# Early split weights and first taps on ScalarE, the first token tile routed ahead, and router scores issued in small steps between expert rows

## What is computed

```python
hn = rms_norm(h, norm_mix_g);  proj = hn @ w_in
xv, bg, cg, ga, gg = split(proj)
y_sc = bg * causal_conv3(cg * xv)                               # 3 taps
y_cf = silu(layer_norm(causal_conv31(ga * sigmoid(gg)) + b))    # 31 taps
h = h + concat(rms_norm(y_sc), rms_norm(y_cf)) @ w_out
hn = rms_norm(h, norm_ffn_g)
q  = hn @ peer_w_q                       # 8 heads of 256
s1, s2 = q[:, :128] @ K1.T, q[:, 128:] @ K2.T     # 128 scores each, per head
idx, gates = top16 of (top16(s1) + top16(s2)), softmax
h = h + sum over 8 heads x 16 of  gelu(u[idx] . hn) * gates * v[idx]
x = final_norm(h)
# second block: ffn1, two attention mixers with gates, ffn2, in fp32
```

## Time and profile before

| | |
|---|---|
| median of 3 runs | 2622.81 us (2619.71 to 2624.23) |
| profiled execution, its own time | 2621.03 us |
| span of that execution, first to last instruction | 2619.2 us |
| granted TensorE clock, mean | 0.913 |
| busy: PE, DVE, ACT, POOL | 83%, 69%, 45%, 29% of the span |
| DMA moved | 758.77 MB, mean 290 GB/s |

### The profile page before, as it was taken

The page is one execution under the profiler, slowest core; times in us unless marked ns, Lnnn a source line. Parts: engine busy times, 40 slices in busy tenths (PEclk is TensorE's granted clock), DMA queues, the critical chain, the costliest instruction groups (busy, mean ns, idle before and its releaser), DMA issues.

```text
span 2619.2 us, 28482 instructions
## 1 busy us (share of the span) xinstructions
PE 2164.6 (83%) x9496; PEld 1516.6 (58%) x9496; DVE 1808.6 (69%) x3312; ACT 1172.9 (45%) x3766; POOL 765.1 (29%) x634
## 2 busy tenths in 40 slices
PE   6986988877777776999674588799919998899999
PEld 6965433332222223885332477588419977698997
DVE  5995366568988886786798987667574545556554
ACT  4223344556666665332354653333244435344443
POOL 0000253444555555333444643333320001100000
PEclk9988999999999998999785579899969998899999
DMA  4220698899999999999997999999974542115453
GB/s 169 81 81 32 235 374 353 319 363 421 421 421 421 408 420 375 389 421 387 374 371 271 367 374 421 378 419 421 392 310 144 181 176 107 65 65 193 145 179 143
DMA packets 107170, 758.77 MB, mean 290 GB/s; under 512 B 12032, under 2 KB 12800, under 8 KB 16400
## 3 DMA queue, kind: packets, MB, share of 16 engines
q0 software_dynamic: 73728, 536.90, 50.7%
q1 hardware_dynamic: 33296, 220.05, 22.3%
HBM read 754.81 MB, written 2.10 MB: 289 GB/s over the span
## 4 chain that ended last, share of the span: by engine, by line
PE 40%; DVE 11%; DMA 4%; issue 3%; ACT 1%; POOL 1%; DVEq 0%; ACTq 0%
PE bank L541 39%; DVE resid L942 4%; DMA pair<-in_uv,idx 4%; DVE pair L1504 2%; DVE half L936 1%; DVE tmp L936 1%; PE bank L902 0%; PE bank L561 0%; DVE smalls L1220 0%; ACT frow L1577 0%; ACT half L1577 0%; DVE smalls L1293 0%; DVE ft_lo L936 0%; POOL smalls L2014 0%; DMA raw<-in_wts 0%
## 5 line engine op out<-in xcount | busy, mean ns | idle before, releaser
L2058 POOL DMA_INDIRECT pair<-in_uv,idx x512 | 654.8, 1279 | 933.9 <-DVE resid L942 588.7
L1577 ACT ACTIVATE smalls<-smalls 128x1 f32<-128x1 f32 x2058 | 540.1, 286 | 660.1 <-DVE smalls L1504 642.2
L1504 DVE CUSTOM_DVE_ANT_0 pair<-pair,hn 128x1024 f32<-128x1024 f32 x512 | 624.3, 1220 | 177.2 <-DMA pair<-in_uv,idx 175.6
L541 PE MATMUL bank<-pair,diag 128*128 128x512 f32 x960 | 480.2, 637 | 158.7 <-ACT diag L1577 158.4
L541 PEld LDWEIGHTS bank<-pair,diag 128*128 128x128 f32 x960 | 175.3, 197 | 459.8 <-ACT diag L1577 320.0
L942 DVE SCALAR_TENSOR_TENSOR resid<-pair,smalls,resid 128x1024 f32<-128x1024 f32 x272 | 348.1, 1280 | 46.4 <-ACT smalls L1577 46.2
L541 PE MATMUL bank<-ft,raw 128*128 128x256 f32 x1664 | 366.1, 384 | 11.9 <-DVE ft L936 11.9
L541 PEld LDWEIGHTS bank<-ft,raw 128*128 128x128 f32 x1664 | 320.5, 193 | 57.3 <-issue 12.7
L936 DVE TENSOR_TENSOR half<-raw,half 128x1024 fp32r<-128x1024 f32 (+1 forms) x212 | 244.5, 1195 | 135.6 <-ACT half L1577 135.6
L541 PE MATMUL bank<-ft_hi,half 128*128 128x256 f32 x1664 | 299.4, 282 | 6.4 <-DVE ft_lo L936 6.4
L1577 ACT ACTIVATE half<-raw 128x1024 fp32r<-128x1024 f32 (+1 forms) x212 | 207.7, 1030 | 164.8 <-PE bank L541 156.8
(11 more groups left out here) (252 smaller groups left out, 2587.4 us busy)
## 6 DMA issues: line engine op xcount, KB each, us to landing
raw<-in_wts SPq DMA_DIRECT2D x194, 1024.0 KB
pair<-in_uv,idx POOLq DMA_INDIRECT x512
raw<-in_wts SPq DMA_DIRECT2D x10, 512.0 KB
raw<-in_wts SPq DMA_DIRECT2D x4, 720.0 KB
resid<-in_x SPq DMA_DIRECT2D x4, 512.0 KB, 5.7
out<-resid SPq DMA_DIRECT2D x8, 256.0 KB, 6.2
raw<-in_wts SPq DMA_DIRECT2D x2, 768.0 KB
rowt<-in_rows SPq DMA_DIRECT2D x1, 1076.0 KB, 12.6
```

The costliest lines, as they stand in the source:

```text
L541: return e.matmul(o, a, b, start=start, stop=stop)
L1504: e.tensor_tensor_reduce(b[:, 0:1024], b[:, 0:1024], HN[i // 128], 1.0, 0.0, ALU.mult, ALU.add, actv[:, i % 8:i % 8 + 1]).then_inc(dotted, 1)
L1577: return e.activation(o, i, f, **kw)
L2058: e.indirect_dma_start(pair[i % NPAIR], None, uv, bass.IndirectOffsetOnAxis(ap=idx[:, n % SLOTS, k:k + 1], axis=0)).then_inc(pairs_in[i % ...
```

## The change

- `half` has four buffers while chunks 0 to 7 are split. Chunks 1, 2 and 3 are split ahead of the first gated product, and chunk 13 ahead of the variance.
- The first tap of each of the eight convolution pieces is done by ScalarE (`tap`).
- The `y_cf` products, the sum into `resid` and the norm of tile 0 stand first; tiles 2 and 3 follow the route of head 0.
- `CALLS`: heads 0 and 1 for tile 0 alone before row 0; heads 2 to 7 for all tiles; then heads 0 and 1 for tiles 1 to 3, for which two weight chunks (`wr`, the same data as `wq` 0 and 1) are loaded a second time.
- `scores_in_steps(n + 2)` runs in step n, for n from 0 to 7: on PE 2 of its matmuls follow each of rows 0 to 7, and the key products rows 10 and 11; ScalarE's four copies follow rows 5, 9, 13 and 14.
- One route a step until step 7 (it was 5), two in steps 8 to 15, none in 16 and 17, one in 18 to 24 (it was 18 to 22). In steps 0 to 7 a route starts at row 2 of its step.
- Every fourth row is added by VectorE until row 127 (it was 95).

```diff
-ON_PE = [i < HALF + 8 and not (i < 96 and i % 4 == 3) for i in range(PAIRS)]
+ON_PE = [i < HALF + 8 and not (i < 128 and i % 4 == 3) for i in range(PAIRS)]
-    ROUTES.append(list(range(_at, min(32, _at + (1 if _n < 6 else 2 if _n < 16 else 0 if _n < 18 else 1)))))
+    ROUTES.append(list(range(_at, min(32, _at + (1 if _n < 8 else 2 if _n < 16 else 0 if _n < 18 else 1)))))
+ROUTE_AT = [2 if _n < 8 else 0 for _n in range(32)]
-CALLS = [(0, 0, 1), (1, 0, NT), (0, 1, NT)] + [(h, 0, NT) for h in range(2, 8)]
+CALLS = [(0, 0, 1), (1, 0, 1)] + [(h, 0, NT) for h in range(2, 8)] + [(0, 1, NT), (1, 1, NT)]
+CALL_KEYS = [("wq", h) for h in range(8)] + [("wr", h) for h in range(2)]
+        hbufs += [ar(f"early{i}", 17968 + 4096 * i, 4096, R).rearrange("p (s n) -> p s n", s=2) for i in range(2)]
-            return hbufs[s % 2]
+            return hbufs[s % 4 if s < 8 else s % 2]
...
             y_cf_part(0)
             mean_squares("ms_cf", 0, (0,), 0, 8)
-            mean_squares("ms_cf", 1, (1, 2, 3), 1, 8)
             y_cf_part(1)
-            y_cf_part(2)
...
                 turned_rows("hn", "hn", t, HN[t])
                 if t == 0:
-                    y_cf_part(3, (0,))
+                    mean_squares("ms_cf", 1, (1, 2, 3), 1, 8)
                     taken(e, "hn", 1)
                     e.wait_ge(keys_in, 16)
-                    scores(0, lambda: y_cf_part(3, (1,)))
+                    scores(0, lambda: y_cf_part(2, (0,)))
+                    y_cf_part(2, (1,))
+                    y_cf_part(3)
             taken(e, "hn", 7)
             scores(1)
-            scores(2)
...
             for i in range(PAIRS):
-                if i % 16 == 0 and i // 16 < 6:
-                    scores(i // 16 + 3)
+                if i % 16 == 0:
+                    steps = scores_in_steps(i // 16 + 2) if i < 128 else iter(())
                 if ON_PE[i]:
                     add_row(i)
+                next(steps, None)
...
+            for s in range(1, 4):
+                split(s)
             for ct in range(4):
...
-                split(ct + 2)
-                pump(12 if ct else 8)
+                split(ct + 4)
+                pump(12 if ct else 11)
...
+            split(13)
             o, out_ = filled(e, "var", 0)
             ts(rstd, o[:], 1.0, EPS, ALU.mult, ALU.add).then_inc(out_, 1)
-            split(13)
...
             gates(0)
+            for t in (2, 3):
+                row_squared(t)
+            for t in (2, 3):
+                row_turned(t)
             scores(1)
-            scores(2)
             first = Paced(chain("A"))
             for n in range(32):
-                if n < 6:
-                    scores(n + 3)
+                steps = scores_in_steps(n + 2) if n < 8 else iter(())
```

More of the change, by code:

```diff
@@ L166, in plan_banks @@
     p.add("var", [1])
-    p.add("ms_cf", [6, 1])
+    p.add("ms_cf", [6, 7])
     p.add("y_cf", [4, 5, 2, 3, 6, 7, 4, 5])
@@ L214, in chunk_ends @@
             ends[key] = (name, 2 * c + 1)
-        elif name == "wq":
-            ends[key] = ("q", 2 * CALL_OF[c, NT - 1] + 1)
+        elif name in ("wq", "wr"):
+            ends[key] = ("q", 2 * CALL_KEYS.index(key) + 1)
         elif name in ("f1", "f2"):
@@ L449, in half, with half_was @@
         def half(s):
-            return hbufs[s % 2]
+            return hbufs[s % 4 if s < 8 else s % 2]
+        def half_was(s):
+            return s - 4 if s < 10 else s - 2
         def halves_of(s, k, kt, sl, n=2048):
@@ L668, in scores @@
                         ins = mm(o[:, cut], wv[:, kt, s * P:(s + 1) * P], HT[:, kt, cut], kt == 0, kt == 7)
-                    ins.then_inc(done, 1)
-                between()
+                        if kt == 7:
+                            ins.then_inc(done, 1)
+                        if kt % 2:
+                            yield
+                for _ in range(2):
+                    yield
                 for s in range(2):
@@ L676, in scores @@
                     ins.then_inc(done, 1)
+                    yield
+            def scores(c, between=lambda: None):
+                for step, _ in enumerate(scores_in_steps(c)):
+                    if step == 7:
+                        between()
             for t in range(NT):
@@ L978, in norm @@
                 for i in range(len(sizes) + 2):
+                    if i == 4:
+                        split(0)
                     if i < len(sizes):
@@ L997, in vector, with conv @@
             e.tensor_copy(maskb[:], maskf[:]).then_inc(masks, 1)
-            def conv(dst, src, wname, k, ct, base_, bias, ready, after=None):
+            def conv(dst, src, wname, k, ct, base_, nth, after):
                 w0 = COLS[wname][0] + ct * k
[L1002 to L1007, removed]
+                for j in range(1, k):
+                    if j == 1:
+                        e.wait_ge(first_tap, nth)
                     else:
                         mine()
-                        ins = stt(dst, s, w, dst, ALU.mult, ALU.add)
-                    if j == k - 1 and after is not None:
+                    ins = stt(dst, src[:, ct, base_ + j:base_ + j + 512], colt[:, w0 + j:w0 + j + 1], dst, ALU.mult, ALU.add)
+                    if j == k - 1:
                         ins.then_inc(after, 1)
@@ L1015, in conv @@
                     yield
[L1017 to L1021, removed]
+            taps = [conv(acc[:, ct, :], upad, "cf", 31, ct, 16, ct + 1, taps_done) for ct in range(4)]
             def pump(n):
@@ L1538, in vector @@
                 row_out(t)
-            first = Paced(chain("A"))
+            first, steps = Paced(chain("A")), iter(())
             for n in range(32):
                 for k in range(16):
-                    if k % 8 == 0:
+                    if k % 8 == ROUTE_AT[n]:
                         steps = route(ROUTES[n][k // 8]) if k // 8 < len(ROUTES[n]) else iter(())
@@ L1583, in rounded @@
                     e.wait_ge(w_in[c.slot], c.landed)
-                    if s >= 2:
-                        through(e, SPLITS[s - 2].key)
+                    if half_was(s) >= 0:
+                        through(e, SPLITS[half_was(s)].key)
                     for m in range(2):
@@ L1887, in chain, with scores_in_steps @@
                 yield from ffn(2, p, mixers_done)
-            def scores(c):
+            def scores_in_steps(c):
                 h, a, b_ = CALLS[c]
@@ L1901, in scores @@
                         ACT.Copy).then_inc(out_, 1)
+                    yield
+            def scores(c):
+                for _ in scores_in_steps(c):
+                    pass
             def row_squared(t):
@@ L1915, in scalar @@
             row_squared(0)
+            row_turned(0)
             row_squared(1)
-            row_turned(0)
             scores(0)
-            row_squared(2)
-            row_squared(3)
-            for t in range(1, NT):
-                row_turned(t)
+            row_turned(1)
             def gates(n):
@@ L2028, in chain @@
                 yield from rates("2" + p)
-            for t in range(NT):
-                rate("hn", t)
+            rate("hn", 0)
+            y_rate("ms_cf", 1, 5, 8)
+            rate("hn", 1)
             def final_rate(t):
@@ L2059, in pool @@
                     ap=idx[:, n % SLOTS, k:k + 1], axis=0)).then_inc(pairs_in[i % NPAIR], 16)
-                if k == 1:
+                if k == (4 if n == 0 else 1):
                     gates(n)
+                if i == 2:
+                    for t in (2, 3):
+                        rate("hn", t)
                 if i > 128 and i % 128 == 11:
```

64 lines of the change are left out of this document (43 added, 21 removed).

## The result

The kernel after takes 2555.59 us (median of 4 runs, 2551.99 to 2559.03) against 2622.12 us (4 runs): a ratio of 0.9746, 95% interval 0.9733 to 0.9759. 2562 was predicted, in a range of 2541 to 2594. The profiled execution has a span of 2553.9 us where it was 2619.2, so 65.3 us are gone.

| | before | after | earlier by | predicted |
|---|---|---|---|---|
| mean of the layer norm | 195.15 | 190.37 | 4.8 | 3.5 |
| indices of step 0 written | 255.07 | 240.76 | 14.3 | 13 |
| PE's first addition | 306.98 | 258.09 | 48.9 | 46 |
| row 16 | 339.8 | 296.7 | 43.1 | 43 |
| row 128 | 675.3 | 596.4 | 78.9 | 74 |

A forecast was written before the change was run, and what follows sets the result against it. PE and VectorE bound the front, then DMA from row 96 to 256, with gathers held back in rows 16 to 96. Terms -43 - 31 + 0 + 13 = -61 us gave 2560 us profiled, 2562 median; range 2541 to 2594.

The forecast's parts named there:

- Front: Up to the layer norm's mean: 11 us less in VectorE's queue, of which 3.5 us arrive at the mean.
- Tile 0's order: Ahead of the rows: with tile 0 first, the scores of head 0 come 8 us sooner.
- First gather and row 0: Start of the rows: first gather near 243 us, PE's first addition at 260.5 against 306.98, -46 us.
- Rival 3: Start of the rows: not started sooner, gains 33 instead of 43 us, 2572 us; chance 0.09.
- Step 0: Rows up to 16: carrying 16.0 us of scores gives back 3 us, so row 16 is 43 us early.
- Rows 16 to 128: Seven steps, DMA-bound at 43.5 us each, take 304.5 us instead of 335.5: -31 us.
- Rival 1: Rows 16 to 128: the steps don't even out, 45 to 48 us a step, 2583 us; chance 0.16.
- Late routes: Routes 30 and 31, landing in steps 23 and 24, cost +13 us, between 8 and 18.6.
- Rival 2: Steps 23 and 24: the late routes are free, nothing is given back, 2549 us; chance 0.12.
- Clock: PE's granted clock: near 1.00 before row 256, against 0.93 in rows 16 to 96.
- Rival 4: Rows 16 to 128: small pieces lower PE's clock; at 0.6 a step is 65.7 us, 2717 us; chance 0.03.
- the first term: Start up to row 16: -43 us, from -46 at row 0 with 3 us taken back.

The follow-up runs named there:

- experiment 6: Kernel after with only split 13 back behind the variance; 2560.32 us, measured once.
- experiment 7: Kernel after with the taps moved from between the four gate products to behind them; 2551.31 us, ratio 0.9723 to the kernel before.
- experiment 5: Kernel after with the whole front edit undone, tile 0's new order and the steps kept; 2567.13 us, ratio 0.9791 to the kernel before.
- experiment 1: Kernel after with each head's scores again as one block ahead of its step; 2614.67 us, ratio 0.9975 to the kernel before.
- experiment 4: Kernel after with six buffers for the gathers instead of seven; 2603.79 us, ratio 0.9933 to the kernel before.
- experiment 2: Kernel after with routes 25 and 26 in steps 16 and 17, none left for steps 23 and 24; 2545.90 us, ratio 0.9714 to the kernel before.
- experiment 3: Kernel after with PE adding every row from row 96 on; 2557.15 us, ratio 0.9751 to the kernel before.
- experiment 9: Kernel after with PE adding every row before 264; 2562.64 us, ratio 0.977 to the kernel before.

## Why the prediction was right

- **Front.** The mean came 4.8 us earlier (3.5 predicted; 4.1 to 6.1 in the six executions with this front), split 13 brought its 1.5 (experiment 6), and PE's first product starts at 20.27 us ("near 20"). That the `y_sc` products hold most of the 11 us back is shown by experiment 7. Tile 0's order brought the rest, 8.0 us of 14.3, by the difference of indices (14.3) and reciprocal (6.3). It has no experiment of its own, but experiment 5 keeps this order with the old front, and there the indices are written 42.2 us behind the reciprocal, as in the kernel after (42.7) and not as before (50.8). The front's 6.3 us were not confirmed to the microsecond: undone, it costs 11.5 (experiment 5), of which 1.7 is PE's clock, and equal fronts differ by 3.5 us.
- **First gather and row 0.** First gather at 241.88 (243 predicted), eighth at 260.35 (263.5), first addition at 258.09 (260.5). The four gathers that I had at 249 to 255 us, behind the squares of tiles 2 and 3, were issued from 246.84 to 254.07. Rival 3 fell.
- **Step 0.** Row 16 was 43.1 us early, 43 predicted, and that is luck: PE's first addition was 2.9 us earlier than I had it (48.9 for 46), and step 0 gave back 5.8 us, not 3. The 3 us rested on a wrong price besides: PE loses 14 x 1.72 - 20.2 = 3.9 us in rows 0 to 7, not 5.5. A likely reason for the larger give-back, not tested: the kernel before made its first addition with seven gathers already landed, and now DMA has a share of 0.99 from 256.4 to 296.7 us, so row 16 waits for transfers.
- **Rows 16 to 128.** -35.8 us instead of -31: the term was mis-sized. I put 17 loads at 2.53 us and 0.5 us on top, 43.5 us a step; measured were 42.8, of which 42.3 is the 17 loads at 421 GB/s, the lower bound that I had named. PE has more to spare than I had worked out, because a row costs it 1.72 us: 12 x 1.72 + 16.0 = 36.6 us in steps 1 to 5 instead of 39.4. That this is where the missing 0.7 us a step comes from is likely, not shown. That the steps and not the earlier start did it is experiment 1; that the slack of seven buffers is used, and one buffer less isn't enough, experiment 4, though not that it is PE's lag which uses it. Rival 1 fell.
- **Rows 128 to 256.** 323.5 against 324.0 us: 0, as predicted.
- **Late routes.** 13 us predicted, 14.5 measured (6.0 + 8.5), between the bounds of 8 and 18.6, and taken back in experiment 2. Rival 2 fell: DMA's share fell with the steps' length, so gathers did not bound them.
- **Clock.** The granted clock is 0.96 in rows 16 to 128, a little short of the "near 1.00" that I had, and 0.91 with the scores in blocks (experiment 1). Rival 4 fell. The Trainium skill, "TensorE: Matmul & The Clock Gate" (Loop structure matters more than you think), sets matmuls that follow each other back to back against ones that each wait long for DMA and run cold. These rows show little of that loss. PE is busy there for 263.46 of 299.70 us (88%), and with blocks for 208.51 of 253.50 us (82%): the small pieces leave it idle less, not more. The variance products show both levels of the clock behind the same wait (experiment 5).
- **Sum.** -61 predicted, -65.3 measured. The rows from 16 to 128 alone make 4.8 us of the difference; the misses of the sum's other terms, each under 2 us, cancel but for 0.5. Inside the first term, -43, two misses of 2.9 and 2.8 us cancel.

Open stay: what adds 4.5 us between row 0 and row 32 when the front is old (experiment 5) and takes back 4.3 when it is faster (7); why steps 8 and 9 suffer with six buffers (4), and which engine's lag uses the slack of the seven.

## What to carry to other kernels

A block of 16 us on one engine, in front of seven buffers that DMA fills in 17.7 us, costs little on paper and 8 us a step in fact; by my estimate in the prediction the buffers' own way round uses up 11 of the 17.7. The same work in pieces of one row's length left 0.5 us a step above what DMA needs. When work is spread out, something is left over at the end of the table: look where it lands (two routes cost 14.5 us in steps 23 and 24, and about 1 us in steps 16 to 19). And where an engine's product waits for the last of several short instructions, look at what filler stands between them.

## What the runs showed of the hardware

- The busy time of a group of matmuls overstates what it costs in a stream: a row is shown as 1.98 us alone and 1.88 us in a stream, and the next group starts 1.72 us after it. Busy time over count gave 1.95.
- The same eight matmul instructions behind the same wait of 2.6 us took 3.70 us at a granted clock of 1.00 and 5.11 to 5.40 us at 0.69 to 0.72, and this in kernels whose instructions are the same up to that point (3.70 us in experiments 2, 3 and 9, 5.18 and 5.11 us in 1 and 4). What decides it was not found; a change of 2 us in such a place can't be read from one profile.
- A DMA share near 1 is not full bandwidth: with six buffers rows 16 to 128 show a share of 0.99 at 389 GB/s, where the kernel after has 1.01 at 417.
